# Thirteen norms: the inverse root as one power operation on GpSimd instead of a Sqrt on ScalarE and a reciprocal on VectorE

## The chip, the cores and the metric

The kernel runs on one core of a Trainium2 chip. The metric is the device time of one execution in microseconds (us). The engines of the core are TensorE (PE; PEld is its weight load), VectorE (DVE), ScalarE (ACT) and GpSimd (POOL); SyncE (SP) issues the DMAs of the weights. Each engine runs its own program in order, and they meet at semaphores.

## The reference

Two transformer-like blocks on 256 tokens of width 1024, in float32. The first block has a stick-breaking attention beside a latent attention (MLA), then a product-key expert layer (PEER) over 16,384 experts. The second has a differential attention beside a Fourier mixing, a gated feed-forward layer (SwiGLU), a conformer convolution, a second feed-forward layer, and a last norm. What matters here is the norm, which the program computes thirteen times, on 256 to 1024 features:

```python
def rms_norm(x, g):
    xf = x.astype(jnp.float32)
    y = xf * lax.rsqrt(jnp.mean(xf * xf, axis=-1, keepdims=True) + EPS)
    return (y * g.astype(jnp.float32)).astype(x.dtype)
```

Some of them go through `modulate` (y times a gain plus a shift), and one is the layer norm inside the convolution.

## The kernel before, in words

Activations lie feature-major: 128 features on the partitions, 256 tokens (T) along the free dimension, in chunks (`x` has 8 chunks). Weights stream from HBM in tiles of 128x1024 into a ring of four slots. Most products are done in full float32 precision by a split: a weight tile is copied as its high part `wh` by ScalarE (`split_high`, L465), and its rest `wl` is computed by GpSimd or VectorE (`split_low`, L474: tile minus high part). The activations are split the same way into `hh` (ScalarE, L1084) and `hl` (VectorE, L1483). TensorE then sums three products, hh*wh, hl*wh and hh*wl (`split_product`, L651 to L672). GpSimd makes `wl` for the tiles named in `BY_POOL` (L196), always in the order of the tiles; its helper `lows(n, count)` runs such a sequence.

A norm number k goes through four engines:
1. ScalarE squares the source in pieces of two chunks into `sq` (L1056).
2. TensorE multiplies the squares by a matrix of ones (L636), which leaves the sum over the features on every partition of a PSUM bank.
3. VectorE scales the sum and adds EPS into `ms`, 128x256 (L1448). ScalarE takes the Sqrt into `rms` (`rootof`, L1064). VectorE takes the reciprocal into `rinv` (L1450).
4. VectorE applies it: `apply` (L1459) is one instruction per chunk with source, gain and `rinv`; `modulate` is four products with `rinv` over two chunks each (L1469) and eight scalings with gain and shift (L1474). ScalarE and VectorE then make `hh` and `hl` of it, and TensorE begins the next product.

Norm 0 is at the start, 1 to 3 between the two parts of the first block's attention, 4 and 5 around its output projection, 6 and 7 at the start of the second block (7 is that of the context, whose residual `hcl` GpSimd makes at L1921), 8 before the first feed-forward layer, 9 before the first product of the convolution, 10 inside it, 11 before the second feed-forward layer, 12 at the end. In step 3 of norms 5, 6, 8, 9 and 11, ScalarE has already issued the high parts of the next stage's first two tiles (`first_highs`) when it comes to the Sqrt, and GpSimd may make their `wl` as soon as these are there. Before the feed-forward layer GpSimd also clears a padded buffer (L1946) and builds diagonal matrices for the convolution (L1932).

ScalarE's functions come from tables, of which one set is active at a time; the program has an ACT_TABLE_LOAD where the set changes, in the trace with the line of the instruction that it is for.

The order of work is written out by hand for each engine. Around the change:

Of the kernel before, what the change touches and what calls it, by code (L numbers as in the profile page):

```python
# [29 lines left out]
ALU = mybir.AluOpType  # L30
ACT = mybir.ActivationFunctionType
# [6 lines left out]
P = 128  # L38
T = 256
# [7 lines left out]
ATT = 3 * P  # L47
# [152 lines left out]
def split_no(n):  # L200

    return sum(t[0] in BY_POOL + BY_DVE for t in TILES[:n])
# [10 lines left out]
def at(it, per, value, n):  # L213

    v = value(n)
    return v if it is None else it * (value(n + per) - v) + v
# [14 lines left out]
def bank_fills(name):  # L231
# [7 lines left out]
          ("pw1_b", 16), ("dw_w", 8 * CONV), ("dw_b", 8), ("ln_g", 8), ("ln_b", 8), ("pw2_b", 8),  # L239
          ("final_g", 8), ("cc", 16), ("lambdas", 4), ("q_norm", 96), ("k_norm", 96), ("fw", 128)]  # L240
CONSTS = [("ident", 128), ("ones", 128), ("iota", 128), ("ntri", 128), ("nones", 128),
          ("mask", ATT), ("invf", 16), ("sel", 2)]
CONSTS2 = [("cos", T), ("sin", T), ("dc", 128), ("ds", 128), ("ct", 2 * T), ("nst", 2 * T)]

# [8 lines left out]
def build(nc, d):  # L254

    with ExitStack() as ctx:
        def sb(name, shape, dt=F32):
            return ctx.enter_context(nc.sbuf_tensor(name, shape, dt))

        def sem(name):  # L260
            return ctx.enter_context(nc.semaphore(name))
# [20 lines left out]
        ms = sb("ms", [P, T])  # L282
        rms = sb("rms", [P, T])
        rinv = sb("rinv", [P, T])
# [13 lines left out]
        def con(name):  # L298
            return cst[:, co[name][0]:co[name][1]]

        ident, ones, iota = con("ident"), con("ones"), con("iota")
        ntri, nones, mask = con("ntri"), con("nones"), con("mask")
# [106 lines left out]
        root = sem("root")  # L409
        normed = sem("normed")  # L410
# [40 lines left out]
        def use(n, k):  # L451
            return n % k, n // k
# [14 lines left out]
        def split_low(eng, n, it=None, per=0):  # L467

            q = split_no(n)
            eng.wait_ge(high_ready, at(it, per, split_no, n) + 1)  # L470
            if q >= 2:
                eng.wait_ge(tile_used, at(it, per, split_no, n) - 1)
            mine = low_by_pool if TILES[n][0] in BY_POOL else low_by_dve
            eng.tensor_tensor(wl[:, q % 2, :], ring[:, n % NS, :], wh[:, q % 2, :], ALU.subtract)\  # L474
                .then_inc(mine, 1)
# [24 lines left out]
        def drained(eng, name):  # L500

            b, u = use(GROUP_NO[name], NB)
            eng.wait_ge(bank_drained[b], u + 1)
# [535 lines left out]
        def _(act):  # L1039
            st = Steps(act, act_step)  # L1040
            A = nc.scalar.activation
# [17 lines left out]

                return lambda q: act.wait_ge(x_added, n + step * (q + 1))  # L1060

            def rootof(k):
                drained(act, ("norm", k))
                A(rms[:, :], ms[:, :], ACT.Sqrt).then_inc(root, 1)  # L1064

            act.wait_ge(small_loaded, 48)
            norm(0, x[:, :, :], KC, [(x_loaded, 16)])
            rootof(0)
            split_high(0)
            split_high(1)  # L1070
            A(csil[:, :, :].rearrange("p k (r n) -> p k r n", n=2),
# [91 lines left out]
            act.wait_ge(act_step, st.n)  # L1163
            drained(act, ("in", 8))
            norm(1, cq[:, :, :], 3, [], prev=("norm", 0))
            rootof(1)
            norm(2, ckv[:, :, :], 2, [], prev=("norm", 1))
            rootof(2)
            drained(act, ("o", 3))
            norm(3, sbT[:, :, :], 4, [], prev=("norm", 2))  # L1170
            rootof(3)
            for hf in range(2):
                for tb in range(TB):
                    ps = full(act, ("uq", tb, hf))
# [39 lines left out]
                    drains(A(mlaT[:, c, :], ps[:, 0:T], ACT.Copy), ("mo", c))  # L1214
            drained(act, ("mo", 3))
            norm(4, mlaT[:, :, :], 4, [], prev=("norm", 3))
            rootof(4)

            norm(5, x[:, :, :], KC, [], prev=("norm", 4), piece_ready=lambda q: drained(act, ("wo", q)))
            first_highs("pq", 0)  # L1220
            rootof(5)
            h_highs(5, 1)
            for c in range(8):
                highs_after(("pq", 2 * c), ("pq", 2 * c + 1))
# [87 lines left out]

            norm(6, x[:, :, :], KC, [], prev=("g", T // GB - 1), piece_ready=added(0))
            first_highs("eq", 0)
            rootof(6)
            h_highs(6, 2)
            for c in range(3):
                highs_after(("eq", 2 * c), ("eq", 2 * c + 1))
# [5 lines left out]
            highs_after(("ef", 0), ("ef", 1))  # L1324
            ps = full(act, ("f", 0))
            drains(A(fT[:, :, :], ps[:, :].rearrange("p (h t) -> p h t", h=2), ACT.Copy), ("f", 0))
            rootof(7)
            for tb in range(TB):
                ps = full(act, ("fy", tb))
                drains(A(Y[:, tb, :], ps[:, :], ACT.Copy), ("fy", tb))  # L1330
# [73 lines left out]

            norm(8, x[:, :, :], KC, [], prev=("norm", 7), piece_ready=lambda q: drained(act, ("eo", q)))
            first_highs("a", 0, 0)
            rootof(8)
            h_highs(8, 3)
            ffn(0)

            norm(9, x[:, :, :], KC, [], prev=("norm", 8), piece_ready=added(X_ADDS["peer"], 2))
            first_highs("pw1", 0)
            rootof(9)
            h_highs(9, 4)
            pb = par("pw1_b")
            for c in range(8):
# [7 lines left out]
                drains(A(cv[:, c, :], ps[:, 0:T], ACT.Identity, bias=par("dw_b")[:, c:c + 1]), ("conv", c))  # L1424
            act.wait_ge(centred, 1)
            norm(10, xc[:, :, :], KC, [], prev=("norm", 9))
            rootof(10)
            act.wait_ge(normed, 11)
            A(cv[:, :, :], xc[:, :, :], ACT.Silu).then_inc(silued, 1)
            norm(11, x[:, :, :], KC, [], prev=("norm", 10), piece_ready=added(X_ADDS["ffn0"]))  # L1430
            first_highs("a", 1, 0)
            rootof(11)
            h_highs(11, 5)
            ffn(1)
            norm(12, x[:, :, :], KC, [], prev=("norm", 11), piece_ready=added(X_ADDS["pw2"], 2))
            rootof(12)

        @block.vector
        def _(dve):  # L1440
            V = nc.vector
            st = Steps(dve, dve_step)
            TT, TS, STT = V.tensor_tensor, V.tensor_scalar, V.scalar_tensor_tensor

            def norm(k, n=D):

                ps = full(dve, ("norm", k))
                drains(TS(ms[:, :], ps[:, 0:T], 1.0 / n, EPS, ALU.mult, ALU.add), ("norm", k))  # L1448
                dve.wait_ge(root, k + 1)
                st.do(V.reciprocal(rinv[:, :], rms[:, :]))  # L1450

            def quarters(dst, ins, c):

# [445 lines left out]

        @block.gpsimd  # L1900
        def _(pool):
            def lows(n, count):

                with pool.Fori(0, count // 4) as it:
                    for i in range(4):
                        split_low(nc.gpsimd, n + i, it, 4)
                for i in range(count - count % 4, count):
                    split_low(nc.gpsimd, n + i)

            split_low(nc.gpsimd, 0)  # L1910
            split_low(nc.gpsimd, 1)
            lows(2, 16)
            lows(TILE_NO["pq", 0], 16)
            lows(TILE_NO["u", 0], J)

            pool.wait_ge(x_added, X_ADDS["peer"])
            pool.dma_start(a3["cst2"], d["consts2"]).then_inc(late_loaded, 16)  # L1917
            pool.dma_start(a3["ctx"], d["ctx"]).then_inc(late_loaded, 16)
            lows(TILE_NO["eq", 0], 8)
            pool.wait_ge(hc_high, 1)  # L1920
            nc.gpsimd.tensor_tensor(hcl[:, :, :], hc, hch[:, :, :], ALU.subtract).then_inc(hc_low, 1)  # L1921
            lows(TILE_NO["ek", 0], 12)

            drained(pool, ("eo", 3))

            dw = par("dw_w").rearrange("p (c k) -> p c k", c=KC)
            pieces = [(i, k, min(k + 4, CONV)) for i in range(len(PE_CONV)) for k in range(0, CONV, 4)]

            def diagonal(n):
                for _ in range(min(n, len(pieces))):  # L1930
                    i, k0, k1 = pieces.pop(0)
                    nc.gpsimd.tensor_tensor(  # L1932
                        diag[:, i, k0:k1, :], ident.unsqueeze(1).broadcast_to([P, k1 - k0, P]),
                        dw[:, PE_CONV[i], k0:k1].unsqueeze(2).broadcast_to([P, k1 - k0, P]),
                        ALU.mult).then_inc(diagonals, 1)

            def ffn(layer):
                def step(f, it=None):
                    for what in ("a", "b"):
                        split_low(nc.gpsimd, TILE_NO[what, layer, f], it, 3 * FF_UNROLL)  # L1940
                    if layer == 0 and it is None:
                        diagonal(3)

                over_ff(pool, step)

            nc.gpsimd.memset(a4["up"], 0.0).then_inc(padded, 1)  # L1946
            diagonal(6)
            ffn(0)
            assert not pieces
            lows(TILE_NO["pw1", 0], 16)  # L1950
            ffn(1)

def constants():

    f = np.float32
    p = np.arange(P)
    t = np.arange(T)
    c = {"ident": np.eye(P), "ones": np.ones((P, P)), "iota": np.broadcast_to(p, (P, P)),  # L1960
         "ntri": -(p[:, None] > p[None, :]).astype(f), "nones": -np.ones((P, P)),
         "mask": np.concatenate([p[:, None] < t[None, :], (p[:, None] + P) < t[None, P:]], 1),
         "sel": p[:, None] % 32 == np.arange(2)}
    inv = f(1.0) / np.power(f(10000.0), np.arange(16, dtype=f) * f(2.0 / 32))
    c["invf"] = np.broadcast_to(inv.astype(f), (P, 16))
    c1 = np.concatenate([np.asarray(c[n], f) for n, _ in CONSTS], 1)

    inv = np.power(f(10000.0), -np.arange(0, 32, 2, dtype=f) / f(32)).astype(f)
    ang = np.concatenate([(t // 64).astype(f)[:, None] * inv, (t % 64).astype(f)[:, None] * inv], 1)
    cos, sin = np.cos(ang).T, np.sin(ang).T  # L1970
    c = {"cos": np.concatenate([cos] * 4), "sin": np.concatenate([-sin, sin] * 2)}
    a = 2 * np.pi * np.outer(np.arange(64), np.arange(64)) / 64
    c["dc"] = np.kron(np.eye(2), np.cos(a) / 8)
    c["ds"] = np.kron(np.eye(2), np.sin(a) / 8)
    a = 2 * np.pi * (np.outer(t, t) % T) / T
    for n, m in (("ct", np.cos(a) / 16), ("nst", -np.sin(a) / 16)):
        c[n] = m.reshape(TB, P, T).transpose(1, 0, 2).reshape(P, TB * T)
    c2 = np.concatenate([np.asarray(c[n], f) for n, _ in CONSTS2], 1)
    return np.ascontiguousarray(c1), np.ascontiguousarray(c2)
# [75 lines left out]
```

## Time and profile before

| | |
|---|---|
| median of 3 runs | 2144.74 us (2136.93 to 2148.17) |
| profiled execution | 2148.26 us, its span 2146.5 us |
| TensorE busy | 1892.4 us, 88% of the span, 15218 matmuls |
| VectorE busy | 1002.9 us, 47% |
| ScalarE busy | 923.0 us, 43% |
| GpSimd busy | 747.9 us, 35% |
| HBM read | 310 MB, 145 GB/s over the span |

The span is the time from the first to the last record of one profiled execution. A share says how busy an engine is on average, not whether something waits for it; that is in the chain of waits, which is followed back from the last instruction.

### The profile page before, as it was taken

Reading aid. Unit: us, or ns where it says so; the run is one execution under the profiler, and the core shown is the slowest. Engines: PE = TensorE matmul, PEld = TensorE weight load, DVE = VectorE, ACT = ScalarE, POOL = GpSimd, SP = SyncE. Lnnn points to the kernel's source line nnn. Section 1 sums busy time; section 2 is a strip of 40 time slices with the busy share of each in tenths; the row PEclk is TensorE's granted clock in tenths of the full one; section 3 lists DMA queues with packets and bytes.
Section 4 is the critical chain, followed back from the end, with each engine's and each line's share of the span. In section 5 each row is a group of like instructions: output and inputs, shape, how many; then the busy total and the mean of one; then the engine's idle time right before and its main releaser. Section 6 shows DMA issues by size and latency. Waiting matters only on the chain.

```text
span 2146.5 us, 40204 instructions
## 1 busy us (share of the span) xinstructions
PE 1892.4 (88%) x15218; PEld 1791.8 (83%) x15218; DVE 1002.9 (47%) x1819; ACT 923.0 (43%) x1431; POOL 747.9 (35%) x318
## 2 busy tenths in 40 slices
PE   6985789999999987799999978996699976978997
PEld 6962589999999976799999978983699976758997
DVE  2035315691000299955555554126444447724444
ACT  4461335555555566544444443224144442014443
POOL 4300047988788500000000015300375555004553
PEclk9886899999999989999999998998899998989999
DMA  4461045445455456655555552200255533024553
GB/s 163 149 249 49 20 142 172 167 166 176 158 185 180 170 198 216 217 180 182 184 180 183 182 187 79 76 24 1 98 176 177 185 119 127 0 84 143 186 185 109
DMA packets 85337, 312.61 MB, mean 146 GB/s; under 512 B 9600, under 2 KB 9600, under 8 KB 84864
## 3 DMA queue, kind: packets, MB, share of 16 engines
q1 hardware_dynamic: 84960, 309.40, 42.4%
q0 software_dynamic: 288, 1.97, 0.2%
q8 instruction: 64, 1.05, 0.2%
q14 instruction: 25, 0.20, 0.0%
HBM read 310.28 MB, written 1.05 MB: 145 GB/s over the span
## 4 chain that ended last, share of the span: by engine, by line
PE 82%; DVE 6%; issue 5%; ACT 3%; POOL 2%; DMA 1%; SPq 0%; POOLq 0%; DVEq 0%; ACTq 0%
PE psr L658 40%; PE acc L658 23%; PE psr L647 4%; PE psr L886 3%; PE acc L714 2%; POOL wl L474 2%; PE psr L1017 2%; PE psr L636 2%; DMA ring<-in_ada_w 1%; DVE rinv L1450 1%; PE acc L722 1%; PE psr L951 1%; DVE sq L1469 1%; ACT wh L465 1%; DVE sq L1474 1%
## 5 line engine op out<-in xcount | busy, mean ns | idle before, releaser
L474 POOL TENSOR_TENSOR wl<-ring,wh 128x1024 fp32r<-128x1024 f32 x286 | 709.9, 2485 | 704.5 <-ACT wh L465 704.3
L465 ACT ACTIVATE wh<-ring 128x1024 fp32r<-128x1024 f32 x458 | 482.2, 1054 | 559.2 <-PE psr L658 498.3
L658 PE MATMUL psr<-hh,wh 128*128 128x256 f32 x2200 | 551.4, 287 | 66.0 <-DVE hl L1483 63.2
L658 PE MATMUL psr<-hl,wh 128*128 128x256 f32 x2200 | 549.7, 286 | 0.0
L658 PEld LDWEIGHTS psr<-hh,wh 128*128 128x128 f32 x2200 | 430.5, 196 | 69.1 <-issue 65.4
L658 PEld LDWEIGHTS psr<-hl,wh 128*128 128x128 f32 x2200 | 430.7, 196 | 0.0
L658 PE MATMUL psr<-hh,wl 128*128 128x256 f32 x2200 | 313.3, 286 | 9.7 <-POOL wl L474 9.7
L474 DVE TENSOR_TENSOR wl<-ring,wh 128x1024 fp32r<-128x1024 f32 x172 | 213.4, 1241 | 184.8 <-ACT wh L465 184.8
L658 PEld LDWEIGHTS psr<-hh,wl 128*128 128x128 f32 x2200 | 287.2, 194 | 12.2 <-POOL wl L474 12.1
L658 PE MATMUL acc<-hl,wh 128*128 128x256 f32 x1024 | 252.4, 284 | 0.0
L658 PE MATMUL acc<-hh,wl 128*128 128x256 f32 x1024 | 252.3, 284 | 0.0
L658 PEld LDWEIGHTS acc<-hl,wh 128*128 128x128 f32 x1024 | 197.6, 193 | 0.0
L658 PEld LDWEIGHTS acc<-hh,wl 128*128 128x128 f32 x1024 | 197.6, 193 | 0.0
L1917 POOL DMA_DIRECT2D arena<-in_consts x1 | 0.7, 722 | 539.2 <-DVE x L1741 539.2
L1687 DVE TENSOR_SCALAR sq<-cst,rT 128x128 f32<-128x128 f32 x256 | 73.2, 375 | 186.7 <-PE psr L658 186.7
L658 PE MATMUL acc<-hh,wh 128*128 128x256 f32 x1024 | 144.1, 283 | 0.8 <-DVE hl L1721 0.8
L1292 ACT ACTIVATE hh<-arena 128x256 fp32r (+1 forms) x128 | 53.4, 417 | 192.9 <-PE acc L658 192.9
L658 PEld LDWEIGHTS acc<-hh,wh 128*128 128x128 f32 x1024 | 132.3, 192 | 0.9 <-DVE ada L1668 0.9
L1816 DVE TENSOR_TENSOR fgl<-arena,fgh 128x256 fp32r<-128x256 f32 x44 | 94.8, 2154 | 42.8 <-ACT fgh L1399 42.8
L647 PE MATMUL psr<-arena,ring 128*128 128x256 f32 x384 | 89.9, 399 | 27.3 <-DVE arena L1791 12.9
L647 PEld LDWEIGHTS psr<-arena,ring 128*128 128x128 f32 x384 | 77.2, 202 | 40.4 <-DVE arena L1791 13.8
L886 PE MATMUL psr<-sq 128*128 128x128 f32 x512 | 76.3, 297 | 37.7 <-issue 35.2
(269 smaller groups left out, 2529.0 us busy)
## 6 DMA issues: line engine op xcount, KB each, us to landing
ring<-in_peer_u SPq DMA_DIRECT2D x128, 512.0 KB, 3.2
ring<-in_peer_v SPq DMA_DIRECT2D x128, 512.0 KB, 3.2
ring<-in_ada_w SPq DMA_DIRECT2D x96, 512.0 KB, 4.2
ring<-in_ffn_a SPq DMA_DIRECT2D x44, 512.0 KB, 4.0
ring<-in_ffn_b SPq DMA_DIRECT2D x44, 512.0 KB, 3.3
ring<-in_ffn_d SPq DMA_DIRECT2D x44, 512.0 KB, 3.2
ring<-in_pw SPq DMA_DIRECT2D x24, 512.0 KB, 3.2
ring<-in_w_in SPq DMA_DIRECT2D x18, 512.0 KB, 3.6
```

The source lines that it names most:

```text
L465: nc.scalar.activation(wh[:, q % 2, :], ring[:, s, :], ACT.Copy).then_inc(high_ready, 1)
L474: eng.tensor_tensor(wl[:, q % 2, :], ring[:, n % NS, :], wh[:, q % 2, :], ALU.subtract)\
L636: last = mm(ps[:, 0:T], ones, sq[:, c * T:(c + 1) * T], start=(c == 0), stop=(c == n - 1))
L647: last = mm(ps[:, m * T:(m + 1) * T], w[:, k, :], src[:, k, :], start=(k == 0), stop=(k == KC - 1))
L658: return mm(out, w, a, start=start, stop=stop, skip_group_check=True)
L714: last = mm(acc[2 + pair % 2][32 * g:32 * g + 32, m * P:(m + 1) * P], csil[:, 2 * g + kk, :], w[:, 2 * g + kk, :], start=(kk == 0), stop=( ...
L722: last = mm(acc[0][:, n:n + 2], rows[:, pair % 2, m * P:(m + 1) * P], con("sel"), start=True, stop=True, skip_group_check=True)
L886: last = mm(ps[:, g * P:(g + 1) * P], oneA[:, c % 2, g, :], oneB[:, c % 2, g, :], start=True, stop=True)
L1017: last = mm(ps[:, 0:T], diag[:, PE_CONV.index(c), k, :], upad[:, c, k:k + T], start=(k == 0), stop=(k == CONV - 1))
L1292: A(hh[:, j % KC, :], part, ACT.Copy).then_inc(c_high, 1)
L1687: ins = TS(oneA[:, b, g, :], iota, rT[:, 0, bass.ds(t + g, 1)], rT[:, 2, bass.ds(t + g, 1)], ALU.is_equal, ALU.mult)
L1816: TT(fgl[:, f % 2, :], fg[:, f % 2, :], fgh[:, f % 2, :], ALU.subtract).then_inc(fg_low, 1)
```

## The change

On ScalarE `rootof` goes, with its thirteen calls. On VectorE `norm(k)` still makes `ms`, then waits for the same semaphore `root`, and has no reciprocal. GpSimd gets a `rootof(k)`, which waits until `ms` is there and until the norm before has been applied (`rinv` is free), and then raises `ms` to the power -0.5 in one tensor_tensor, the second operand being a constant column broadcast over the tokens. Its calls are placed in GpSimd's order: norm 0 ahead of the first two `lows`, norms 1 to 5 ahead of those of the query projection ("pq"), 6 ahead of those of "eq", 7 behind them, 8 ahead of the diagonals and the first feed-forward layer, 9 ahead of "pw1", 10 and 11 ahead of the second feed-forward layer, 12 last. The constants get one more column.

```diff
-CONSTS = [..., ("mask", ATT), ("invf", 16), ("sel", 2)]
+CONSTS = [..., ("mask", ATT), ("invf", 16), ("sel", 2), ("power", 1)]
...
 @block.scalar
-            def rootof(k):
-                drained(act, ("norm", k))
-                A(rms[:, :], ms[:, :], ACT.Sqrt).then_inc(root, 1)
...            (and the calls rootof(0) to rootof(12))
 @block.vector
                 drains(TS(ms[:, :], ps[:, 0:T], 1.0 / n, EPS, ALU.mult, ALU.add), ("norm", k))
                 dve.wait_ge(root, k + 1)
-                st.do(V.reciprocal(rinv[:, :], rms[:, :]))
...
 @block.gpsimd
+            def rootof(k):
+
+                drained(pool, ("norm", k))
+                if k:
+                    pool.wait_ge(normed, k)
+                nc.gpsimd.tensor_tensor(rinv[:, :], ms[:, :], con("power").broadcast_to([P, T]), ALU.pow).then_inc(root, 1)
+
...
+            rootof(0)
             split_low(nc.gpsimd, 0)
             split_low(nc.gpsimd, 1)
             lows(2, 16)
+            for k in range(1, 6):
+                rootof(k)
             lows(TILE_NO["pq", 0], 16)
...
+            rootof(6)
             lows(TILE_NO["eq", 0], 8)
+            rootof(7)
             pool.wait_ge(hc_high, 1)
...
             nc.gpsimd.memset(a4["up"], 0.0).then_inc(padded, 1)
+            rootof(8)
             diagonal(6)
             ffn(0)
             assert not pieces
+            rootof(9)
             lows(TILE_NO["pw1", 0], 16)
+            rootof(10)
+            rootof(11)
             ffn(1)
+            rootof(12)
...
-         "sel": p[:, None] % 32 == np.arange(2)}
+         "sel": p[:, None] % 32 == np.arange(2), "power": np.full((P, 1), -0.5)}
```

## Rows read from the trace of the kernel before

**Rows 1.** The chain that ended last, shares by engine and by line.
```profile
PE 82%; DVE 6%; issue 5%; ACT 3%; POOL 2%; DMA 1%; SPq 0%; POOLq 0%; DVEq 0%; ACTq 0%
PE psr L658 40%; PE acc L658 23%; PE psr L647 4%; PE psr L886 3%; PE acc L714 2%; POOL wl L474 2%; PE psr L1017 2%; PE psr L636 2%; DMA ring<-in_ada_w 1%; DVE rinv L1450 1%; PE acc L722 1%; PE psr L951 1%; DVE sq L1469 1%; ACT wh L465 1%; DVE sq L1474 1%
```

**Rows 2.** Instructions by line: duration in ns min/median/max, first and last start.
```profile
L1448 DVE TENSOR_SCALAR ms<-psr x13: 418/425/425, 15.8 to 2136.2; 128x256 f32<-128x256 f32 x13
L1064 ACT ACT_TABLE_LOAD  x8: 1283/1283/1283, 10.4 to 2134.6; - x8
L1450 DVE RECIPROCAL rinv<-rms x13: 1753/1753/1754, 16.7 to 2137.1; 128x256 f32<-128x256 f32 x13
```

**Rows 3.** Timeline at norm 0 (start, us, engine, line), and L1459 by line.
```profile
15.79 0.42 DVE L1448 TENSOR_SCALAR ms<-psr 128x256 f32<-128x256 f32 x1 [7.42 <-PE psr L636]
16.25 0.42 ACT L1064 ACTIVATE rms<-ms 128x256 f32<-128x256 f32 x1 [4.55 <-DVE ms L1448]
17.69 4.82 POOL L474 TENSOR_TENSOR wl<-ring,wh 128x1024 fp32r<-128x1024 f32 x2 [17.23 <-ACT wh L465]
18.49 6.68 DVE L1459 SCALAR_TENSOR_TENSOR sq<-x,prm,rinv 128x256 f32<-128x256 f32 x8
...
L1459 DVE SCALAR_TENSOR_TENSOR sq<-x,prm,rinv x24: 472/474/2556, 18.5 to 2141.6; 128x256 f32<-128x256 f32 x24
```

**Rows 4.** Timeline at norm 9: `ms`, and the two parts of `modulate`.
```profile
1747.91 0.42 DVE L1448 TENSOR_SCALAR ms<-psr 128x256 f32<-128x256 f32 x1 [2.25 <-PE psr L636]
...
1751.77 2.66 DVE L1469 TENSOR_TENSOR sq<-x,rinv 128x512 f32<-128x512 f32 x4
1754.36 2.66 DVE L1474 TENSOR_SCALAR sq<-sq,gsc,ada 128x256 f32<-128x256 f32 x8
```

**Rows 5.** Timeline at norm 6: `ms` and the end of `modulate`.
```profile
1277.61 0.42 DVE L1448 TENSOR_SCALAR ms<-psr 128x256 f32<-128x256 f32 x1 [2.80 <-PE psr L636]
...
1283.51 2.66 DVE L1474 TENSOR_SCALAR sq<-sq,gsc,ada 128x256 f32<-128x256 f32 x8
```

**Rows 6.** Timeline at norm 11, the same two.
```profile
1928.59 0.42 DVE L1448 TENSOR_SCALAR ms<-psr 128x256 f32<-128x256 f32 x1 [2.87 <-PE psr L636]
...
1934.34 2.66 DVE L1474 TENSOR_SCALAR sq<-sq,gsc,ada 128x256 f32<-128x256 f32 x8
```

**Rows 7.** GpSimd's instructions by shape: count, busy us, mean ns, idle before.
```profile
L474 POOL TENSOR_TENSOR wl<-ring,wh 128x1024 fp32r<-128x1024 f32 x286 | 709.9, 2485 | 704.5 <-ACT wh L465 704.3
```

**Rows 8.** Timeline at norm 5: GpSimd's subtractions, `ms`, and the apply.
```profile
285.15 4.65 POOL L474 TENSOR_TENSOR wl<-ring,wh 128x1024 fp32r<-128x1024 f32 x2 [198.09 <-ACT wh L465]
286.15 0.42 DVE L1448 TENSOR_SCALAR ms<-psr 128x256 f32<-128x256 f32 x1 [2.76 <-PE psr L636]
...
288.84 4.01 DVE L1459 SCALAR_TENSOR_TENSOR sq<-x,prm,rinv 128x256 f32<-128x256 f32 x8
```

**Rows 9.** Timeline at norm 12: the apply.
```profile
2138.87 3.25 DVE L1459 SCALAR_TENSOR_TENSOR sq<-x,prm,rinv 128x256 f32<-128x256 f32 x8
```

**Rows 10.** Timeline at norm 8: GpSimd's diagonals, and the scalings of `modulate`.
```profile
1531.97 6.92 POOL L1932 TENSOR_TENSOR arena<-cst,prm 128x512 f32<-128x512 f32 x6
1532.53 0.42 DVE L1448 TENSOR_SCALAR ms<-psr 128x256 f32<-128x256 f32 x1 [2.58 <-PE psr L636]
...
1542.12 6.64 DVE L1474 TENSOR_SCALAR sq<-sq,gsc,ada 128x256 f32<-128x256 f32 x8
1544.36 2.96 POOL L1932 TENSOR_TENSOR arena<-cst,prm 128x512 f32<-128x512 f32 x3
```

**Rows 11.** GpSimd's instructions by shape, behind norm 7.
```profile
L1921 POOL TENSOR_TENSOR hcl<-arena,hch 128x2048 fp32r<-128x2048 f32 x1 | 5.2, 5246 | 15.3 <-ACT hch L1332 15.3
```

**Rows 12.** Timeline at norms 1 to 3 and the head norms after them.
```profile
168.48 3.75 PE L636 MATMUL psr<-sq,cst 128*128 128x256 f32 x8 [1.84 <-ACT sq L1056]
...
180.67 1.76 DVE L1566 TENSOR_TENSOR arena<-arena 128x1536 f32<-128x1536 f32 x1 [4.03 <-ACT arena L1175]
...
193.98 0.22 ACT L1186 ACTIVATE small<-small 128x16 f32<-128x16 f32 x1
```

More of the change, by code:

```diff
@@ L241 @@
 CONSTS = [("ident", 128), ("ones", 128), ("iota", 128), ("ntri", 128), ("nones", 128),
-          ("mask", ATT), ("invf", 16), ("sel", 2)]
+          ("mask", ATT), ("invf", 16), ("sel", 2), ("power", 1)]
 CONSTS2 = [("cos", T), ("sin", T), ("dc", 128), ("ds", 128), ("ct", 2 * T), ("nst", 2 * T)]
@@ L1060, in added @@
                 return lambda q: act.wait_ge(x_added, n + step * (q + 1))
-            def rootof(k):
-                drained(act, ("norm", k))
-                A(rms[:, :], ms[:, :], ACT.Sqrt).then_inc(root, 1)
             act.wait_ge(small_loaded, 48)
             norm(0, x[:, :, :], KC, [(x_loaded, 16)])
-            rootof(0)
             split_high(0)
@@ L1165, in _ @@
             norm(1, cq[:, :, :], 3, [], prev=("norm", 0))
-            rootof(1)
             norm(2, ckv[:, :, :], 2, [], prev=("norm", 1))
-            rootof(2)
             drained(act, ("o", 3))
             norm(3, sbT[:, :, :], 4, [], prev=("norm", 2))
-            rootof(3)
             for hf in range(2):
@@ L1216, in _ @@
             norm(4, mlaT[:, :, :], 4, [], prev=("norm", 3))
-            rootof(4)
             norm(5, x[:, :, :], KC, [], prev=("norm", 4), piece_ready=lambda q: drained(act, ("wo", q)))
             first_highs("pq", 0)
-            rootof(5)
             h_highs(5, 1)
@@ L1314, in _ @@
             first_highs("eq", 0)
-            rootof(6)
             h_highs(6, 2)
@@ L1326, in _ @@
             drains(A(fT[:, :, :], ps[:, :].rearrange("p (h t) -> p h t", h=2), ACT.Copy), ("f", 0))
-            rootof(7)
             for tb in range(TB):
@@ L1406, in _ @@
             first_highs("a", 0, 0)
-            rootof(8)
             h_highs(8, 3)
@@ L1412, in _ @@
             first_highs("pw1", 0)
-            rootof(9)
             h_highs(9, 4)
@@ L1426, in _ @@
             norm(10, xc[:, :, :], KC, [], prev=("norm", 9))
-            rootof(10)
             act.wait_ge(normed, 11)
@@ L1431, in _ @@
             first_highs("a", 1, 0)
-            rootof(11)
             h_highs(11, 5)
@@ L1435, in _ @@
             norm(12, x[:, :, :], KC, [], prev=("norm", 11), piece_ready=added(X_ADDS["pw2"], 2))
-            rootof(12)
         @block.vector
```

## The prediction

> **What bounds the kernel now.** I read the chain of waits first. It gives TensorE 82% of the span, VectorE 6%, and by line the reciprocal of the norms 0.8% and the products at L658 63% [rows 1]. So the kernel is a chain of matmul stages, and each norm is a joint at which TensorE stands still. Then I read the instructions of the norm by line: thirteen times a scaling out of PSUM (`ms`, 0.42 us), a reciprocal on VectorE (1.75), and eight loads of an activation table of 1.28 us [rows 2]; the Sqrt between them takes 0.42 in norm 0. The reader is to see that nothing in a norm is large, but everything in it is serial. Last I read the timeline around each norm, for what GpSimd does there.
>
> **What is removed.** In norm 0 `ms` ends at 16.21 (15.79 and 0.42) and the first instruction that uses `rinv` starts at 18.49: 2.28 us for Sqrt, reciprocal and three handoffs [rows 3]. Where the Sqrt waited for its table load too it was more: in norm 9 `ms` ends at 1748.33 `modulate` begins at 1751.77 and its two parts end at 1757.02 [rows 4], 3.4 us of joint instead of 2.3. Norms 6 and 11 lie between: from `ms` to the end of `modulate` they take 8.14 and 7.99 us against norm 9's 8.69 [rows 5, 6].
>
> **What is added.** One power instruction of 128x256 on GpSimd with duration d, and two handoffs, for which I take 0.1 us (the Sqrt starts 0.04 us after `ms` ends in the timeline of norm 0). No row shows a power. The nearest row on GpSimd is the subtraction of 128x1024, 2.485 us [rows 7], so a pass over 256 elements is 0.62 us. That is the lower end, if the power costs no more than a pass. A power is a logarithm, a product and an exponential, and GpSimd would do them in software. VectorE's reciprocal, one iterated function, costs 4.1 of VectorE's own passes (1753 over 425 ns) [rows 2]. I take ten passes for log, product and exp, d = 6.2 us; as ends of the range two passes, 1.2 us, and twenty-four, 15 us. This is an estimate, and it is the number on which the forecast hangs.
>
> **What moves on GpSimd's queue.** The change puts the power ahead of the residual subtractions (`lows`) of the stage's first two tiles. Now those run early, under `ms`, Sqrt and reciprocal: in norm 5 from 285.15 to 289.80, and only their last 0.96 us lies beside the eight apply instructions, which take 4.01 us instead of the 3.25 that they take in norm 12, where GpSimd is idle [rows 8, 9]. In norm 0 both subtractions lie beside the apply, and it takes 6.68: one VectorE instruction gets through per GpSimd instruction, and the longest takes 2.56 us instead of 0.47 [rows 3]. After the change every norm with `lows` behind its power is as norm 0 is now. The 4.8 us of two subtractions begin when the power ends, VectorE gets two of its instructions done in them, and the rest follows. I count from the end of `ms` to the end of the apply loops:
>
> - Norm 0: now 8.96; then 0.1 + d + 4.82 + six apply instructions of 0.41 = d + 7.37. Difference d - 1.6 [rows 3].
> - Norm 5, same form: now 6.28. Difference d + 1.1 [rows 8].
> - Norms 6, 9, 11 (four products, eight scalings; after two products 3.9 us are left): then d + 8.8. Now 8.14, 8.69 and 7.99 [rows 4 to 6]. Differences d + 0.7, d + 0.1, d + 0.8.
> - Norm 8: GpSimd has six diagonals (6.92), two subtractions (5.5, from 1538.9 to 1544.4) and three diagonals (2.96), and they hold VectorE up already: the scalings take 6.64 us there instead of norm 9's 2.66, and end at 1548.76 [rows 10]. From the end of `ms`, 1532.95, that is 15.8 now; then 0.1 + d + 15.4, as all 15.4 us lie behind the power. Difference d - 0.3.
> - Norms 4, 7, 10 and 12 have nothing right behind their power on GpSimd. All four are on the path: the chain holds 0.8% of reciprocals, which is ten of 1.75 us [rows 1] and leaves out norms 2, 3 and 7, and norm 7 is on it by way of the residual `hcl`, for whose input GpSimd stood idle for 15.3 us [rows 11]. Difference d + 0.1 - 2.27 = d - 2.2 each, -8.7 for four without the d.
>
> TensorE waits for the end of the apply loops in all six of the norms with `lows`, since the residuals `hl` stand behind it on VectorE; the `lows` themselves come in time (4.9 us after the power, while TensorE starts some 9 us after it and needs the first 3 us later still).
>
> Norms 1 to 3 follow one another, and here the change helps a little. ScalarE no longer holds the squares of norms 2 and 3 back behind its Sqrts. The eight matmuls of norm 3 start at 168.48 [rows 12] and could start some 1.8 us earlier; the first apply would end at about 165 + d, so at d = 6.2 it is 1.1 us that is gained. The next use of VectorE's result, L1566, starts at 180.67 and its answer is needed only at 193.98, when ScalarE is done with its evictions; three powers in a row move L1566 to about 168.5 + 3d = 187, still covered (the three instructions there take 3.7 us). Cover ends at d near 7. Against that, the Sqrt at L1186 now has its table from norm 1; it would load it itself, 1.28 us on the path. Together +0.2. The table loads dropped elsewhere lie under waits or are in the differences above.
>
> **Sum.** 10 d - 7.8 + 0.2. With d = 6.2 that is +54.4 us. The profiled execution took 2148.3 (span 2146.5, with 1.8 around it), so it would take 2202.7. The median of the runs is 2144.7, 3.5 lower, so the forecast is 2199. At 1.2 us the sum is +4 and the time 2148; at 15 us it is +142, and norms 1 to 3 lose their cover for some 25 more, 2312.
>
> **The rivals.**
> - Short power: five passes, d = 3.1. Sum +23, 2168. For it speaks that GpSimd's row is bound by fetching two operands, so a longer body need not cost in proportion. Against it, a power of full single precision is not short.
> - Not slower: d under 1.9 us. At 0.62 the sum is 6.2 - 7.8 - 0.5, -2, 2143, within 0.5%. For it speaks nothing but the other GpSimd rows. Note that even then almost nothing is won, as the port takes back in norms 5, 6, 9 and 11 what the shorter joint gives.
> - Faster: the power costs a pass, and VectorE gets ahead of the subtractions or runs beside them at full speed. The place is the apply loops of norms 0, 5, 6, 9 and 11, the price 3.4 us each. Then the differences are -5.0, -2.3, -2.2, -2.8, -2.1, and with -1.8 in norm 8 and -1.6 in four others some -22 us: 2122. It decides from d below about 1.9. The apply of norm 0 speaks against it, since there the price was paid [rows 3].
> - Long power: twenty passes, d = 12.4. 124 - 8, and norms 1 to 3 lose about 15 at L1566: +131, 2276.
> - The power isn't done in vectors but element by element, in which case 16 partitions of a core go one after the other: 16 times 6.2 is 99 us, ten of them on the path and three in a row with some 20 us of cover. +1260, about 3400. Nothing in the rows excludes it.
>
> The Trainium skill, "Advanced Engine Details and Errata", states in its note on VectorE's performance modes that two-port VectorE instructions and GpSimd instructions block each other. The apply loops of norm 0 agree (6.68 against 3.25 us), and norm 8 shows it for the scalings too. If instead GpSimd's waiting subtractions let VectorE through first, the sum would be lower by some 13 us.
>
> **How the numbers follow.** Chances: forecast 0.41, short power 0.15, not slower 0.11, faster 0.06, long power 0.16, element by element 0.11. Range 2147 to 2312: it leaves out element by element (0.11), the faster case (0.06) and the top of the long one (0.03). What this kernel's measurement can tell from no change is about 0.5%, 10.7 us; the sum passes that from d = 1.9. Faster 0.06, within 0.11, slower 0.83.
>
> **What would show it.** In the new profile: a GpSimd row of 128x256 for `rinv` x13 whose mean is d; no Sqrt in the norms, and a table load at L1186's place; from `ms` to the apply, d + 0.1 in each norm. The `lows` begin where the power ends, and the apply instructions of norms 5, 6, 9 and 11 take about 3.5 us more than now. L1566 starts 6 us later with the line after it no later. The forecast is wrong if d isn't near 6; the structure is wrong if ten times d less 7.8 doesn't give the difference, for which the likeliest causes would be VectorE not held up by the subtractions, or held up by the power itself.

## The result: 1.235 times the time before, and one instruction is most of it

The changed kernel takes 2641.6 us (median of 4 runs, 2640.1 to 2655.8) beside 2140.8 for the kernel before; the ratio is 1.235 (95% interval 1.230 to 1.240). The forecast was 2199 with a range up to 2312, so the direction was right and the time 440 us off. The profiled execution took 2640.4 us with a span of 2638.2, 491.7 more than before.

First the page of the changed kernel: busy time by engine, the chain by engine, and the group of the power.

```profile
PE 1872.0 (71%) x15218; PEld 1773.4 (67%) x15218; DVE 1000.0 (38%) x1806; ACT 908.5 (34%) x1410; POOL 1284.9 (49%) x331
...
PE 58%; POOL 22%; issue 13%; DVE 4%; POOLq 2%; ACT 1%; DMA 1%; DVEq 0%; ACTq 0%
...
L1889 POOL TENSOR_TENSOR rinv<-ms,cst 128x256 f32<-128x256 f32 x13 | 534.5, 41119 | 339.3 <-DVE ms L1431 339.3
```

The third line is the answer: the power over 128x256 takes 41.12 us, not 6.2 (d, the duration of one power, in the forecast). GpSimd, 2% of the chain before [rows 1], has 22% of it now. TensorE does the same work in both (15218 matmuls, 1872 us busy beside 1892).

The timelines at norms 5, 9, 8 and 12, in that order (start, us, engine, line). They answer to [rows 8], [rows 4], [rows 10] and [rows 9].

```profile
458.93 0.42 DVE L1431 TENSOR_SCALAR ms<-psr 128x256 f32<-128x256 f32 x1 [2.76 <-PE psr L636]
459.43 41.12 POOL L1889 TENSOR_TENSOR rinv<-ms,cst 128x256 f32<-128x256 f32 x1 [35.95 <-DVE ms L1431]
500.52 4.82 POOL L474 TENSOR_TENSOR wl<-ring,wh 128x1024 fp32r<-128x1024 f32 x2
500.59 7.41 DVE L1441 SCALAR_TENSOR_TENSOR sq<-x,prm,rinv 128x256 f32<-128x256 f32 x8 [41.23 <-POOL rinv L1889]
...
2119.61 6.77 DVE L1451 TENSOR_TENSOR sq<-x,rinv 128x512 f32<-128x512 f32 x4 [41.23 <-POOL rinv L1889]
2126.31 2.66 DVE L1456 TENSOR_SCALAR sq<-sq,gsc,ada 128x256 f32<-128x256 f32 x8
...
1863.32 7.87 POOL L1926 TENSOR_TENSOR arena<-cst,prm 128x512 f32<-128x512 f32 x6
1869.16 10.11 DVE L1456 TENSOR_SCALAR sq<-sq,gsc,ada 128x256 f32<-128x256 f32 x8
...
2630.56 3.26 DVE L1441 SCALAR_TENSOR_TENSOR sq<-x,prm,rinv 128x256 f32<-128x256 f32 x8 [41.23 <-POOL rinv L1889]
```

Read norm 5 from above: `ms` ends at 459.35, the power starts 0.08 later, VectorE waits 41.23 us. GpSimd's two subtractions start in the same moment as the apply, which takes 7.41 us; in norm 12, with nothing behind the power, the same eight instructions take 3.26.

Then norms 1 to 3, which answer to [rows 12]: three powers in a row, the square of the head norm, and ScalarE's table load and Sqrt.

```profile
197.55 41.12 POOL L1889 TENSOR_TENSOR rinv<-ms,cst 128x256 f32<-128x256 f32 x1 [71.42 <-DVE ms L1431]
240.39 41.12 POOL L1889 TENSOR_TENSOR rinv<-ms,cst 128x256 f32<-128x256 f32 x1 [1.73 <-DVE ms L1431]
282.84 41.12 POOL L1889 TENSOR_TENSOR rinv<-ms,cst 128x256 f32<-128x256 f32 x1 [1.33 <-DVE ms L1431]
...
325.58 1.75 DVE L1548 TENSOR_TENSOR arena<-arena 128x1536 f32<-128x1536 f32 x1
...
305.42 1.28 ACT L1178 ACT_TABLE_LOAD   x1
329.36 0.21 ACT L1178 ACTIVATE small<-small 128x16 f32<-128x16 f32 x1 [22.66 <-DVE small L1550]
```

### The profile page after: what moved, and what is told of

Read it like the earlier page. It is cut to its first block, busy times and chain, and to the rows that moved or that the text cites. A ratio compares the mean times of both kernels' runs of the same rounds, so it can differ in the third digit from the quotient of the medians.

```text
span 2638.2 us, 40195 instructions
## 1 busy us (share of the span) xinstructions
PE 1872.0 (71%) x15218; PEld 1773.4 (67%) x15218; DVE 1000.0 (38%) x1806; ACT 908.5 (34%) x1410; POOL 1284.9 (49%) x331
## 3 DMA queue, kind: packets, MB, share of 16 engines
q8 instruction: 64, 1.05, 0.2%
HBM read 310.28 MB, written 1.05 MB: 118 GB/s over the span
## 4 chain that ended last, share of the span: by engine, by line
PE 58%; POOL 22%; issue 13%; DVE 4%; POOLq 2%; ACT 1%; DMA 1%; DVEq 0%; ACTq 0%
PE psr L658 31%; POOL rinv L1889 19%; PE acc L658 18%; PE psr L886 3%; POOL wl L474 2%; PE psr L1017 2%; PE acc L714 2%; POOLq L256 2%; DVE sq L1451 1%; DMA ring<-in_ada_w 1%; DVE sq L1456 1%; DVE sq L1441 1%; PE acc L722 1%; PE psr L636 1%; POOL arena L1926 0%
## 5 line engine op out<-in xcount | busy, mean ns | idle before, releaser
L474 POOL TENSOR_TENSOR wl<-ring,wh 128x1024 fp32r<-128x1024 f32 x286 | 711.5, 2491 | 350.1 <-ACT wh L465 349.9
L1889 POOL TENSOR_TENSOR rinv<-ms,cst 128x256 f32<-128x256 f32 x13 | 534.5, 41119 | 339.3 <-DVE ms L1431 339.3
L474 DVE TENSOR_TENSOR wl<-ring,wh 128x1024 fp32r<-128x1024 f32 x172 | 213.5, 1241 | 183.2 <-ACT wh L465 183.2
L1079 ACT ACTIVATE hh<-sq 128x512 fp32r<-128x512 f32 x24 | 15.1, 630 | 297.6 <-DVE sq L1456 203.3
```

What stands on the lines that cost most here:

```text
L1889: nc.gpsimd.tensor_tensor(rinv[:, :], ms[:, :], con("power").broadcast_to([P, T]), ALU.pow).then_inc(root, 1)
```

## The experiments

The theory after the result: "size only". The power costs 41 us, some fixed price per column, and all other steps of the forecast hold. Its rivals: the long stalls cost more than themselves, or the power's price is a fixed one per instruction; and "no port", that the slow apply loops have another reason than the subtractions.

**1. What a power costs.** The kernel before, with probes on GpSimd where it is idle:

```diff
             lows(2, 16)
+            (src_p: squares of dw_w, 128x128; scr: a scratch tile; pw: the constant -0.5)
+            st.do(G(scr[:, 0:128], src_p[:, 0:128], pw.broadcast_to([P, 128]), ALU.pow))
+            st.do(G(scr[:, 0:32], ...)) ; [:, 0:1] ; [0:16, 0:128] ; [0:1, 0:128]
+            and 32 columns of ones, with exponent 1, and of the integers
```

> The kernel before, with ten probes on GpSimd in the idle time behind its first residuals (some 80 us, off the path, nothing else changed): multiply and subtract of 128x128; powers with exponent -0.5 of 128x128, 128x32, 128x1, 16x128 and 1x128; and powers of 128x32 with other values (all ones; integers 1 to 32 by partition constants; exponent 1). Theory 'vectors': a core of GpSimd handles its 16 partitions at once and the power costs 160 ns per column whatever the partitions: 20.6 us for 128 columns with 128, 16 and 1 partition alike, 5.2 for 32, under 1 us for one column. Rival 'element by element': 16x128 takes 20.6 as 128x128 does, but 1x128 a sixteenth, 1.3 us. Rival 'fixed price' (the instruction fetches something each time): 32 columns take far more than a quarter of 128. Rival 'by value': ones or exponent 1 are much cheaper. Span as before, 2146 us within 10.

The timeline of GpSimd in that kernel, from the subtraction of 128x128 on:

```profile
87.07 0.41 POOL L1920 TENSOR_TENSOR scr<-src_p,prm 128x128 f32<-128x128 f32 x1
87.56 20.75 POOL L1921 TENSOR_TENSOR scr<-src_p,cst 128x128 f32<-128x128 f32 x1
108.39 5.42 POOL L1922 TENSOR_TENSOR scr<-src_p,cst 128x32 f32<-128x32 f32 x1
113.89 0.55 POOL L1923 TENSOR_TENSOR scr<-src_p,cst 128x1 f32<-128x1 f32 x1
114.52 20.73 POOL L1924 TENSOR_TENSOR scr<-src_p,cst 16x128 f32<-16x128 f32 x1
135.33 20.71 POOL L1925 TENSOR_TENSOR scr<-src_p,cst 1x128 f32<-1x128 f32 x1
156.11 5.43 POOL L1926 TENSOR_TENSOR scr<-cst 128x32 f32<-128x32 f32 x1
161.62 5.43 POOL L1927 TENSOR_TENSOR scr<-src_p,cst 128x32 f32<-128x32 f32 x1
167.13 5.41 POOL L1928 TENSOR_TENSOR scr<-cst 128x32 f32<-128x32 f32 x1
```

From 1 to 128 columns 20.2 us, so 159 ns per column and some 0.4 us once; from 128 to 256 columns (41.12) 159 again. 128, 16 and 1 partition cost the same, and so do ones, an exponent of 1 (read from a full tile and not from a broadcast column) and integers. So the price is one per column, whatever the number of partitions, and the same for all the values that were tried, which are none of them negative. "Element by element", "fixed price" and "by value" fall. Why a column takes 159 ns isn't shown by this; no run looked inside the instruction. The span is 2148.9 in this one execution, beside 2146.5 without the probes.

**2. The change with an operation of one pass in the power's place.** What it leaves out is the norms: `rinv` is -0.5 everywhere.

```diff
-                nc.gpsimd.tensor_tensor(rinv[:, :], ms[:, :], con("power").broadcast_to([P, T]), ALU.pow).then_inc(root, 1)
+                nc.gpsimd.tensor_tensor(rinv (as 2 x 128), ones (broadcast), con("power") (broadcast), ALU.mult).then_inc(root, 1)
```

> The kernel after, with a multiply of two constants in the power's place on GpSimd (0.6 us; rinv becomes -0.5 everywhere, so the norms are left out of the computation). Theory 'size only': the steps of the forecast hold and its sum 10 d - 7.8 with d = 0.6 gives -2 us and perhaps some 1 to 2 more from elsewhere: 2139 beside 2141. The apply loops of norms 0 and 5 take 7.4 us, the four products of norms 6, 9 and 11 take 6.8. Rival 'no port': the apply loops are slow in the kernel after for another reason than the subtractions that start with them; then they take 3.25 and 2.5 us here and the time is near 2119. Rival 'the stalls cost extra': if the 41 us stalls cost more than themselves by TensorE's clock or the ring, this kernel lies well under 2139 too.

Measured: 2137.1 us beside 2146.7, ratio 0.996 (0.994 to 0.997). The operation by line (min/median/max in ns), then the timeline at norm 5:

```profile
L1889 POOL TENSOR_TENSOR rinv<-cst x13: 607/612/614, 16.1 to 2123.8; 128x256 f32<-128x256 f32 x13
```

```profile
280.26 4.82 POOL L474 TENSOR_TENSOR wl<-ring,wh 128x1024 fp32r<-128x1024 f32 x2
280.34 7.40 DVE L1441 SCALAR_TENSOR_TENSOR sq<-x,prm,rinv 128x256 f32<-128x256 f32 x8 [0.72 <-POOL rinv L1889]
```

The apply takes 7.40 us here too, so a long idle isn't what slows it. "No port" falls in its detail, though by the time alone it could not be told, as the -9.6 lies between the two forecasts. By the stages of the profile the ten norms together come to +1.1 us; the rest of the gain lies in stretches between norms, treated below. The sum rule behind the forecast says -1.7 for the ten.

The rival that the long stalls cost more than themselves falls by the profile of the changed kernel. No stretch between two norms is more than 1 us longer there than before. And TensorE comes back no slower: in the 10 us that follow its restart behind norm 5 the mean granted clock is 0.84 of full speed in the changed kernel, from 508.7 us, and 0.76 in the kernel before, from 293.6 us.

**3. The power over 64 of 256 columns** (three quarters of the tokens aren't normed; `rinv` is 0.5 there).

```diff
-                nc.gpsimd.tensor_tensor(rinv[:, :], ms[:, :], con("power").broadcast_to([P, T]), ALU.pow).then_inc(root, 1)
+                nc.gpsimd.tensor_tensor(rinv[:, 0:64], ms[:, 0:64], con("power").broadcast_to([P, 64]), ALU.pow).then_inc(root, 1)
```

> The kernel after, with the power over 64 of the 256 columns (rinv is a constant 0.5 in the others, so three quarters of the tokens aren't normed). Theory 'size only' with 160 ns per column: d = 10.3 us, and 10 d - 7.8 + 0.5 for norms 1 to 3 (cover ends near 7, so they lose about 8 more) gives +103 and norms 1 to 3 some +8, about 2250; some us less where the other stages gain by the stalls. Rival 'fixed price': d well above 10.3, time above 2300.

Measured: 2253.8 us, ratio 1.049 (1.046 to 1.053), and the power by line:

```profile
L1889 POOL TENSOR_TENSOR rinv<-ms,cst x13: 10522/10522/10555, 15.9 to 2235.0; 128x64 f32<-128x64 f32 x13
```

The time is within 4 us of the 2250 that was expected, but not by the parts that were expected. In the profile the ten norms come to +100.3 us, where the rule says +97.4 for d = 10.52 (the expectation's "+103" is ten times d without the -7.8). Norms 1 to 3, from the end of norm 1's `ms` to the transposes at L810, take 67.2 us beside 49.4 before: +17.8, and not the 8 that were expected. The span grew by 106.7, as the stretches between the norms are 11.4 us shorter; that they make up for it is luck. What norms 1 to 3 wait for is in the rows, first of the kernel before, then of this one:

```profile
172.03 7.99 PE L791 MATMUL psr<-ring,arena 128*128 128x384 f32 x24
...
197.17 10.24 PE L791 MATMUL psr<-ring,arena 128*128 128x384 f32 x24 [16.81 <-DVE arena L1441]
220.35 1.28 ACT L1178 ACT_TABLE_LOAD   x1
221.64 0.22 ACT L1178 ACTIVATE small<-small 128x16 f32<-128x16 f32 x1
```

TensorE's products at L791 wait for the apply of norm 2 (`pe.wait_ge(normed, 3)`), ScalarE's evictions follow them, and then the head norms' Sqrt, here with its table load. Two powers in a row lie ahead of all that. From the end of norm 1's `ms` to that Sqrt it is 48.3 us here and 30.5 before.

**4. The power in norms 1 to 3 alone.**

```diff
+            for k in range(1, 4):       (GpSimd, behind lows(2, 16))
+                drained(pool, ("norm", k)); pool.wait_ge(normed, k); (the power)
-            rootof(1), rootof(2), rootof(3)     (ScalarE), and the reciprocals of these three
```

> The kernel before, with the power on GpSimd in norms 1, 2 and 3 alone, Sqrt and reciprocal in the ten others. Theory: three powers in a row of 41.1 us less some 22 us of cover, +101, 2242. Rival 'all in the sum': the cover isn't there, and +117 (three times 39) comes, 2258.

Measured: 2247.3 us beside 2147.3, ratio 1.046 (1.043 to 1.049), so +100. From the end of norm 1's `ms` to the start of L810 (the transposes that need the scaled heads) it is 150.8 us here and in the changed kernel, 49.4 before: +101.4 in both, for powers of 123.4. At this d the 22 us of cover are real, and "all in the sum" falls.

**5. Residuals held back behind the power.**

```diff
                 nc.gpsimd.tensor_tensor(rinv[:, :], ms[:, :], ..., ALU.pow).then_inc(root, 1)
+                if k in TURN:                              # {0: 0, 5: 1, 6: 2, 9: 4, 11: 5}
+                    pool.wait_ge(h_low, 4 * TURN[k] + 4)
```

> The kernel after, where GpSimd holds the residuals behind the powers of norms 0, 5, 6, 9 and 11 until VectorE has made the hl of the norm. Theory 'port': the apply of norms 0 and 5 falls from 7.41 to 3.25 us and the products of 6, 9 and 11 from 6.8 to 2.5; the first residual then comes some 0.8 us late for TensorE; net -3.4 each, -17, 2625. Rival 'no port' (VectorE slow after a long idle, say): apply loops as in the kernel after, and the late residuals add: above 2642.

Measured: 2628.9 us, ratio 1.226 (1.221 to 1.230), against 1.235 (1.230 to 1.240) for the change as it is. The two intervals touch, so the answer is in the stages and not in the times; the spans are 2624.9 and 2638.2. Norm 5 in the timeline, with TensorE's wait for the first residual last:

```profile
501.93 3.25 DVE L1441 SCALAR_TENSOR_TENSOR sq<-x,prm,rinv 128x256 f32<-128x256 f32 x8 [41.23 <-POOL rinv L1891]
507.90 4.71 POOL L474 TENSOR_TENSOR wl<-ring,wh 128x1024 fp32r<-128x1024 f32 x2 [6.00 <-DVE hl L1465]
...
510.32 1.22 PE L658 MATMUL psr<-hh,wl 128*128 128x256 f32 x8 [0.63 <-POOL wl L474]
```

3.25 instead of 7.41, with the same 41 us of idle time ahead of it. The only thing taken away is the work that GpSimd did beside it. That shows the contention: from the end of `ms` to the end of the apply or modulate, norms 0 and 5 fall by 4.2 us and norms 6, 9 and 11 by 4.3, 21 together. TensorE gives 0.4 to 0.8 of it back in each at the first residual. The span falls by 13.3 rather than the expected 17; norm 0 to norm 1 is 3.4 us longer here, a stretch that varies from kernel to kernel (below).

**6. The same lesson on the kernel before.** ScalarE makes the first two high parts ahead of norm 0's Sqrt, and the six diagonals of norm 8 move behind the pw1 residuals.

```diff
+            split_high(0); split_high(1)
             rootof(0)
-            split_high(0); split_high(1)
...
-            diagonal(6)
             ffn(0)
             lows(TILE_NO["pw1", 0], 16)
+            diagonal(6)
```

> The kernel before, with two edits of GpSimd's timing alone: ScalarE makes the first two high parts ahead of norm 0's Sqrt, so that their residuals are done before the apply, and the six diagonals that lie beside norm 8's modulate are built behind the pw1 residuals. Theory 'port': norm 0's apply falls from 6.68 to 3.25 us (-3.4), norm 8's modulate from 13.6 to about 6.8 (-6.8), sum -10, 2131. Rival 'no port': both stay as they are, 2141. Rival 'given back': the diagonals delay the convolution on VectorE by more than its 6 us of slack there and some of the -10 comes back.

Measured: 2141.8 us beside 2146.7, ratio 0.998 (0.996 to 1.000): not told apart from no change by the time. The profile shows the parts, at norm 0 and at norm 8, and then in the convolution behind norm 9, first before and then here:

```profile
17.61 3.25 DVE L1459 SCALAR_TENSOR_TENSOR sq<-x,prm,rinv 128x256 f32<-128x256 f32 x8
...
1523.24 6.28 DVE L1469 TENSOR_TENSOR sq<-x,rinv 128x512 f32<-128x512 f32 x4
1524.59 4.38 POOL L1932 TENSOR_TENSOR arena<-cst,prm 128x512 f32<-128x512 f32 x3
1529.44 2.66 DVE L1474 TENSOR_SCALAR sq<-sq,gsc,ada 128x256 f32<-128x256 f32 x8
...
1787.34 37.09 DVE L1856 SCALAR_TENSOR_TENSOR arena<-arena,prm 128x256 f32<-128x256 f32 x60
...
1769.32 41.45 DVE L1856 SCALAR_TENSOR_TENSOR arena<-arena,prm 128x256 f32<-128x256 f32 x60
1786.39 6.92 POOL L1932 TENSOR_TENSOR arena<-cst,prm 128x512 f32<-128x512 f32 x6
```

Norm 0's apply falls from 6.68 to 3.25 as expected. At norm 8 I missed that three diagonals of the first feed-forward step move up as the six go; they meet the products, which take 6.28 (6.97 before). So norm 8 falls from 15.8 to 11.1 us and not to 9.

And the rival "given back" holds. At their new place the six diagonals run beside the first sixty instructions of VectorE's convolution, which take 41.45 us for 37.09: 4.4 us, nearly all of the 4.7 that norm 8 gains. What is left by these rows is norm 0's 3.4 and 0.3 more, beside a difference of 4.9 in the medians. The contention was moved and not removed.

**7. The Sqrt out of PSUM,** on top of that.

```diff
-                drained(act, ("norm", k))
-                A(rms[:, :], ms[:, :], ACT.Sqrt).then_inc(root, 1)
+                ps = full(act, ("norm", k))
+                if k >= 2:
+                    act.wait_ge(normed, k - 1)
+                drains(A(rms[:, k % 2, :], ps[:, 0:T], ACT.Sqrt, scale=1.0 / NORM_WIDTH[k], bias=con("eps")), ("norm", k))
...
-                drains(TS(ms[:, :], ps[:, 0:T], 1.0 / n, EPS, ALU.mult, ALU.add), ("norm", k))
```

> As the kernel with the freed port, and ScalarE takes the Sqrt straight out of PSUM with the scale and EPS as its scale and bias (no ms instruction on VectorE, two rms buffers). Theory: norms 4, 7, 10, 12 and 0 lose 0.45 us each; in norms 5, 6, 9 and 11 the apply then starts earlier into the residuals still running on GpSimd and gains nearly nothing: -2.5 more, 2128. Rival: all ten gain 0.45, -4.5 more, 2126. Both lie under the kernel before.

Measured: 2129.7 us beside 2146.7, ratio 0.993 (0.990 to 0.995). It beats both kernels, by 0.7% the one before and by some 19% the changed one. The timeline at norm 5:

```profile
278.79 4.65 POOL L475 TENSOR_TENSOR wl<-ring,wh 128x1024 fp32r<-128x1024 f32 x2 [195.72 <-ACT wh L466]
...
279.78 0.47 ACT L1067 ACTIVATE rms<-psr,cst 128x256 f32<-128x256 f32 x1 [0.21 <-PE psr L637]
280.29 1.75 DVE L1453 RECIPROCAL rinv<-rms 128x256 f32<-128x256 f32 x1 [3.27 <-ACT rms L1067]
282.08 4.41 DVE L1462 SCALAR_TENSOR_TENSOR sq<-x,prm,rinv 128x256 f32<-128x256 f32 x8
```

The Sqrt alone takes 0.47 where `ms` and Sqrt took 0.88, and the apply, which starts earlier into the same subtractions, 4.41 instead of 4.01: the 0.4 is given back in this norm, as the theory has it. From the last matmul of the sum to the end of the apply or modulate, norms 0, 4, 7, 10 and 12 are each 0.4 us shorter than in experiment 6, and 5, 6 and 8 not at all; norms 9 and 11 are 0.35 and 1.05 shorter, where the theory had nothing. The span is 3.1 us under that of experiment 6, for 2.5 expected. Between the medians lie 12, more than the edit's rows account for; the last section has a part of the reason.

## Why the prediction was wrong, by its own steps

**The step that failed** is the size of one term: "I take ten passes for log, product and exp, d = 6.2 us", with "twenty-four, 15 us" as upper end. It is 41.12 us, 66 passes. Nothing else is needed for an error of this size. By the forecast's own rule 10 d - 7.8 (its terms add up to -7.9) for the ten norms on the path, against the differences (from the end of `ms` to the end of the apply or modulate) that the profiles show:

| kernel | d, us | ten norms by the rule | ten norms measured |
|---|---|---|---|
| one pass (2) | 0.61 | -1.7 | +1.1 |
| 64 columns (3) | 10.52 | +97.4 | +100.3 |
| the change | 41.12 | +403.4 | +406.2 |

- **Part removed, 2.27 us a norm:** right. Norms 4, 7, 10 and 12 are each 38.96 us longer; d + 0.1 - 2.27 is 38.95.
- **Queue behind the power:** right in kind, and under 0.2 us short in norms 0 and 5, 0.5 to 0.7 in norms 6, 8, 9 and 11. The apply of norm 0 takes 7.41, where I had counted 7.28 (4.82 and six of 0.41); in `modulate` VectorE gets less done beside the two subtractions than I took (6.77 for the four products, where I counted 6.07). Shown by experiments 2 and 5.
- **Norms 1 to 3:** wrong at the forecast's own d, right for a very dear power. "Three in a row with some 20 us of cover" fits: the cover is 22, and the Sqrt's table load at L1178 lies beside a wait of 22.66 us, so it costs nothing. But I had ScalarE's evictions end at their old time, 193.98, and so "cover ends at d near 7" and +0.2 us. I overlooked that the products at L791 wait for norm 2, and that the evictions move with them. On that path experiment 3 has two powers and 27.3 us more up to the Sqrt, and the kernel before 30.5, so the loss is 2 d - 3.2: my estimate for d = 6.2, from these rows, is 9 us. On the path of the third power it is 3 d - 22, by the changed kernel; that one is the longer from a d of about 19. Beside the 440 us the slip is small, and at d = 41 it doesn't show.
- **TensorE waits for the end of the apply loops:** right. In norm 5 it starts 0.75 us after the apply ends in both kernels, and the low parts are in time in the changed kernel.
- **The chances:** the dear case was there with 0.11 ("element by element", 99 us each), for a reason that experiment 1 refutes, and the stretch from 15 to 99 us had none. The bound of 24 passes was mine and no row's: the rows bound the price from below alone. VectorE's reciprocal at 4.1 passes is a row of another engine and another function, and says nothing of GpSimd's power.
- **The Trainium skill,** "GPSIMD Engine Reference", section 3.1, on bodies of three operations and more at roughly 3 operations per cycle, pointed the wrong way here: from it I worked out 2.9 us for 40 operations. At its 1.2 GHz, 159 ns per column would be an estimated 190 cycles, and at its rate room for some 570 operations. The same page calls GpSimd the wrong choice for ordinary elementwise arithmetic, where VectorE is about twice as fast; the trace agrees, with 2.49 us for the subtraction at L474 on GpSimd and 1.24 on VectorE.
- **The port:** the apply has two inputs in SBUF, `x` and `rinv`. The Trainium skill, "Advanced Engine Details and Errata", says in "GPSIMD Details" that GpSimd shares a read and a write interface with VectorE, and that it conflicts with VectorE's instructions in a two-port mode or with two SBUF inputs. The note on performance modes that the prediction names speaks of the two-port ones alone. Experiment 5 agrees: 7.41 against 3.25 us.

The books close thus: ten norms +406.2, norms 1 to 3 +101.4, sum 507.6; the span grew by 491.7. The missing 15.9 are in the stretches between norms. The largest two are norm 0's apply to norm 1's `ms`, 4.9 us shorter, and norm 5 to norm 6 (the query projection and the expert layer), 985.2 before and 980.0 after. The first stretch takes 138.3 us before, 133.4 in the change and 135.9 to 145.3 in the kernels of the experiments, without order in d; in part of it TensorE waits for weights (5.2 us before, 4.0 in the change). The second is below. So no share of the 15.9 is shown to be an effect of the power.

## What to carry to other kernels

The rows of GpSimd's other operations bound the price of a function from below alone: put the instruction beside the kernel once (128x1, 128x32, 128x128) before thirteen copies go on the path. This one costs 0.159 us per column whatever the partitions hold, so it suits a few columns (0.55 us for one) and not 256 columns in which all 128 partitions hold the same. And work that is queued on GpSimd right behind the instruction that releases VectorE runs against what it released: 7.4 us for 3.25 of apply; let it run under the reduction before, or hold it a few us. Look at what it meets at its new place, too: in experiment 6 the six diagonals cost VectorE's convolution 4.4 us. Last, when several instructions in a row get longer, follow each of them to what waits for it, and not only the last one: norm 2 released the products at L791, and that was the longer path at d = 10.5.

## What the runs showed of the hardware that was not expected

The stretch from norm 5 to norm 6 takes either 985 us (the kernel before, and experiments 1 and 4) or 979 to 981 (the change and the others), in kernels that run the same instructions there. The windows of 80 us that begin 545 us before the end of norm 6's `ms` tell where it lies; columns are busy time (and instructions) of PE, PEld, DVE, ACT and POOL, then the mean granted clock of TensorE, DMA share and GB/s. In order: the kernel before, then experiment 4, the change, and experiment 6.

```profile
733.00:813.00 80.00, 65.58 (x775) 59.68 (x775) 69.59 (x173) 49.37 (x136) 2.41 (x2) 0.85 0.54 185
```

```profile
837.70:917.70 80.00, 65.51 (x775) 59.58 (x774) 69.61 (x173) 49.34 (x136) 2.39 (x1) 0.85 0.53 185
```

```profile
943.00:1023.00 80.00, 61.09 (x796) 56.03 (x798) 67.69 (x170) 51.20 (x136) 7.20 (x3) 0.98 0.56 198
```

```profile
721.30:801.30 80.00, 60.69 (x803) 55.42 (x806) 67.67 (x170) 51.91 (x136) 7.90 (x4) 1.00 0.57 200
```

The granted clock is 0.85 of full speed in two of them and 0.98 to 1.00 in the others, with TensorE no more than 82% busy and fewer matmuls done in the same time. In the kernel before it is at half (1.2 of 2.4 GHz) in short pieces there, 742 to 745 us being one, and at full speed between them.

The three kernels with the dip have norm 0 as before, and those without it have another norm 0, 270 us and more ahead. But one profile of each kernel can't tie the dip to the kernel. The 24 executions of the kernel before that ran with experiments 1, 2, 6 and 7 have mean granted clocks from 0.934 to 0.948 and spans from 2153.1 down to 2135.3 us, and the longer ones are in the main those with the lower clock; the profiled one had 0.938. So the clock differs between executions of one and the same program, and what decides it isn't settled.

It bears on the small differences. The four executions of the kernel before with 0.947 or 0.948 have spans of 2135.3 to 2138.7 us. Those of experiment 2 with 0.948 or 0.949 have 2134.3 to 2137.5 us: at about the same clock hardly anything is left of its -9.6. Experiment 6 has 2130.9 to 2133.0 at 0.948 to 0.950, and experiment 7 has 2125.5 to 2127.9 at 0.948 to 0.951, so there they are some 5 and 10 us under the kernel before. Here a difference of under half a per cent is to be read from the stages and from executions of like clock, not from the medians alone.
